# Two attentions of a two-model forward pass: output-weight halves subtracted one step after they are cast, and one chunk's queries turned ahead of the scores

## The reference

```python
def odd_mixer(h_lat, h_ctx, w_in, w_out, sink, cos, sin, ctx_out):
    q, k, v = odd_project(h_lat, w_in)
    qc, kc, vc = odd_project(h_ctx, w_in)
    q = apply_rope(q, cos, sin)
    k = apply_rope(k, cos, sin)
    y, yc = window_gqa_sink(q, k, v, qc, kc, vc, sink, ctx_out)
    return y @ w_out, ((yc @ w_out) if ctx_out else None)
```

## Time and profile before

| | |
|---|---|
| median of 3 runs | 1707.29 us (1706.27 to 1708.68) |
| the profiled execution, its own time | 1701.35 us |
| its span, first to last instruction | 1699.9 us |
| mean granted clock of TensorE | 0.977 |
| TensorE matmuls, busy | 1593.0 us, 94% |
| VectorE, busy | 1049.2 us, 62% |
| ScalarE, busy | 805.3 us, 47% |
| GpSimd, busy | 238.5 us, 14% |
| loads and stores | 257.27 MB, mean 151 GB/s |

### The profile page before, as it was taken

How to read it: one execution, slowest core, us unless ns; L and a number is a source line. 1 busy time by engine, 2 the same in 40 slices (tenths; PEclk the granted TensorE clock), 3 DMA queues, 4 the chain that set the end, 5 groups by cost and what they waited for, 6 DMA issues and landing times.

```text
span 1699.9 us, 26871 instructions
## 1 busy us (share of the span) xinstructions
PE 1593.0 (94%) x10834; PEld 1382.0 (81%) x10834; DVE 1049.2 (62%) x1939; ACT 805.3 (47%) x1514; POOL 238.5 (14%) x284
## 2 busy tenths in 40 slices
PE   5899979999999999979899997888999998899998
PEld 3788758877777888867799986777999887689996
DVE  3633755565354435778787767666677656667765
ACT  1322872433233323558455544555555555556553
POOL 1200430010010100002011101132111012321110
PEclk8999999999999999999999998899999998999999
DMA  9467022262564224020356453324455533245452
GB/s 383 151 255 276 11 71 114 77 254 117 217 253 173 99 99 149 11 91 25 149 178 218 175 189 103 130 95 141 158 190 181 189 133 119 75 155 193 174 209 76
DMA packets 39418, 257.27 MB, mean 151 GB/s; under 512 B 5504, under 2 KB 6784, under 8 KB 10496
## 3 DMA queue, kind: packets, MB, share of 16 engines
q1 hardware_dynamic: 36416, 249.61, 40.4%
q0 software_dynamic: 1296, 4.72, 0.8%
q10 hardware_dynamic: 1584, 1.23, 0.3%
HBM read 254.49 MB, written 1.05 MB: 150 GB/s over the span
## 4 chain that ended last, share of the span: by engine, by line
PE 81%; DVE 9%; ACT 6%; issue 2%; DMA 1%; POOL 1%; SPq 0%; DVEq 0%; ACTq 0%
PE ps L473 24%; PE ps L474 23%; PE ps L475 23%; PE ps L489 2%; PE ps L640 2%; PE ps L627 2%; DVE wl L1709 2%; PE ps L618 2%; ACT wh L1277 1%; ACT arena L1621 1%; PE ps L1043 1%; ACT arena L1348 1%; PE ps L515 1%; DMA raw<-in_ev_w_in 1%; PE ps L599 1%
## 5 line engine op out<-in xcount | busy, mean ns | idle before, releaser
L1709 DVE TENSOR_TENSOR wl<-raw,wh 128x1024 fp32r<-128x1024 f32 (+2 forms) x328 | 383.0, 1209 | 379.5 <-ACT wh L1277 378.9
L1277 ACT CAST wh<-raw 128x1024 fp32r<-128x1024 f32 (+1 forms) x338 | 332.6, 1033 | 517.1 <-PE ps L475 398.5
L473 PE MATMUL ps<-xh,wh 128*128 128x256 f32 (+1 forms) x1582 | 495.4, 313 | 8.3 <-ACT arena L1578 8.0
L474 PE MATMUL ps<-xl,wh 128*128 128x256 f32 (+1 forms) x1582 | 490.0, 310 | 0.0
L475 PE MATMUL ps<-xh,wl 128*128 128x256 f32 (+1 forms) x1582 | 489.9, 310 | 0.0
L473 PEld LDWEIGHTS ps<-xh,wh 128*128 128x128 f32 x1582 | 303.4, 192 | 33.2 <-issue 9.2
L473 PE MATMUL ps<-wh,xh 128*128 128x512 f32 (+2 forms) x844 | 306.6, 363 | 21.6 <-DVE xl L2275 6.8
L475 PEld LDWEIGHTS ps<-xh,wl 128*128 128x128 f32 x1582 | 303.4, 192 | 15.3
L474 PEld LDWEIGHTS ps<-xl,wh 128*128 128x128 f32 x1582 | 303.5, 192 | 15.0 <-issue 0.7
L474 PE MATMUL ps<-wl,xh 128*128 128x512 f32 (+2 forms) x844 | 301.9, 358 | 0.0
L475 PE MATMUL ps<-wh,xl 128*128 128x512 f32 (+2 forms) x844 | 301.7, 357 | 0.0
(11 more groups left out here) (210 smaller groups left out, 1805.0 us busy)
## 6 DMA issues: line engine op xcount, KB each, us to landing
raw<-in_ada SPq DMA_DIRECT2D x48, 1024.0 KB, 6.8
raw<-in_up SPq DMA_DIRECT2D x44, 1024.0 KB, 6.0
raw<-in_fin SPq DMA_DIRECT2D x44, 1024.0 KB, 4.8
raw<-in_down SPq DMA_DIRECT2D x22, 1024.0 KB, 4.9
raw<-in_fout SPq DMA_DIRECT2D x22, 1024.0 KB, 4.9
raw<-in_win SPq DMA_DIRECT2D x12, 1024.0 KB, 4.9
raw<-in_ev_w_in SPq DMA_DIRECT2D x9, 1024.0 KB, 6.7
raw<-in_wout SPq DMA_DIRECT2D x8, 1024.0 KB, 4.8
```

The costliest lines, as they stand in the source:

```text
L473: e.matmul(out, A[0], B[0], start=first, stop=False)
L474: e.matmul(out, A[0], B[1], start=False, stop=False)
L1277: e.copy(hi_of(j)[:, a:b], raw_of(j)[:, a:b]).then_inc(*S.hi.up((j, half)))
L1709: e.tensor_tensor(lo_of(j)[:, a:b], raw_of(j)[:, a:b], hi_of(j)[:, a:b].bitcast(F), ALU.subtract).then_inc(*S.lo.up((j, half)))
```

## The change

In both attentions, ScalarE casts a half of an early output-weight chunk in a step, and VectorE subtracts it in the step after. In the even attention only VectorE's place moves (steps 16, 18, 20, 22). In the odd attention chunks 0 and 1 of `od_w_out` are both split so, cast in steps 4, 6, 8 and 10 and subtracted in 5, 7, 9 and 11. So chunk 0 is no longer split ahead of the loop and chunk 1 no longer whole in step 4. VectorE's diagonals for the gates move to steps 12 and 14.

TensorE turns query chunk 1 before the scores of step 0, and only the product of chunk 3 stays in step 1. The copies of turned chunks 1, 2 and 3 are all made by ScalarE; those of chunk 1 stand before the loop, behind the fifth group of query tiles.

```diff
--- before.py
+++ after.py
@@ -445,7 +445,8 @@
     ATT2 = [Att2(l) for l in range(2)]
 
 
-    EARLY = {15 + 2 * i: (J["ev_w_out", i // 2], i % 2) for i in range(4)}
+    EARLY = {("ev", 15 + 2 * i): (J["ev_w_out", i // 2], i % 2) for i in range(4)}
+    EARLY |= {("od", 4 + 2 * i): (J["od_w_out", i // 2], i % 2) for i in range(4)}
 
 
 
@@ -572,7 +573,7 @@
                 take_turn((key, f))
                 wait_copied(b, (key, f))
 
-        def head_features(key, js, src, toks, wait):
+        def head_features(key, js, src, toks, wait, side=None):
 
             for j in js:
                 b = bank()
@@ -584,6 +585,8 @@
                 m.then_inc(*S.tr.up((key, j)))
                 BANK[key, j] = b
                 take_turn((key, j))
+                if side:
+                    SIDE[key, j] = side
                 wait_copied(b, (key, j))
 
         def gates(key, groups, at):
@@ -871,7 +874,7 @@
         def od_turned(i):
 
             head_features("oqt", [2 * i, 2 * i + 1], lambda t, j: QS1[:, t, 128 * j:128 * j + 128], t2,
-                          [(S.vec, ("oqk", (2 if i == 0 else 4 + 2 * i) + 1))])
+                          [(S.vec, ("oqk", (2 if i == 0 else 4 + 2 * i) + 1))], "act" if i else None)
 
         od_queries(1)
         head_features("okt", range(2), lambda t, j: KS[:, t, j, :, :].rearrange("p two d -> p (two d)"), t4, [(S.vec, ("oqk", 5))])
@@ -884,14 +887,14 @@
         def last_queries(i):
 
             nb[0] = 1
-            if i in (1, 2, 3):
+            if i == 1:
+                od_queries(3)
+            elif i in (2, 3):
                 od_turned(i)
-            if i == 1:
-                nb[0] = 1
-                od_queries(3)
 
         keys = [(S.ea if SIDE.get(("okt", j)) == "act" else S.ev, ("okt", j)) for j in range(2)]
-        span[:] = [6, 2]
+        span[:], nb[0] = [6, 2], 1
+        od_turned(1)
         attention1(ATT["od"], {0: [(S.ea, ("ova", 3)), *keys, *both_copied(0)]} | {4 * i: both_copied(2 * i) for i in (1, 2, 3)},
                    last_queries)
         span[:] = [0, 6]
@@ -1510,8 +1513,8 @@
 
         def first_weights(i):
             copies_vb(copy, 1, {1: (0, 1), 2: (2, 3)}.get(i, ()))
-            if i in EARLY:
-                weights_half(*EARLY[i])
+            if ("ev", i) in EARLY:
+                weights_half(*EARLY["ev", i])
 
         attention1(ATT["ev"], J["ev_w_in", 8], first_weights)
 
@@ -1537,22 +1540,24 @@
         for n, tiles in enumerate(QK1[0:5]):
             for tile in tiles:
                 qk(tile)
-            i = n - 2 if n > 2 else {0: 4, 1: 0}.get(n)
+            i = {0: 4, 1: 0, 3: 1}.get(n)
             if i is not None:
                 weights(after(J["od_w_in", i]))
             if n == 3:
                 copies_heads(copy, "okt", range(2), KT, 512)
                 copies_heads(copy, "oqt", [0, 1], QT1, 256, -0.125, free)
+            if n == 4:
+                copies_heads(copy, "oqt", [2, 3], QT1, 256, -0.125)
 
         def last_queries(i):
             if i == 1:
                 for tile in QK1[5]:
                     qk(tile)
-            elif i == 4:
-                weights(after(J["od_w_in", 3]))
+            elif ("od", i) in EARLY:
+                weights_half(*EARLY["od", i])
 
         def queries_turned(i):
-            if i in (1, 2, 3):
+            if i in (2, 3):
                 copies_heads(copy, "oqt", [2 * i, 2 * i + 1], QT1, 256, -0.125)
 
         attention1(ATT["od"], J["od_w_in", 3], last_queries, queries_turned)
@@ -2169,8 +2174,8 @@
             copies_vb(copy, 1, {1: (0, 1), 2: (2, 3)}.get(i, ()))
             if i in (5, 7, 9, 11):
                 next(diagonals)
-            if i in EARLY:
-                weights_half(*EARLY[i])
+            if ("ev", i - 1) in EARLY:
+                weights_half(*EARLY["ev", i - 1])
 
         attention1(ATT["ev"], beside)
 
@@ -2205,13 +2212,13 @@
                 for tile in QK1[5]:
                     qk(tile)
                     qk_rest()
-            elif i == 4:
-                weights(after(J["od_w_in", 3]))
-            elif i in (6, 8):
+            elif ("od", i - 1) in EARLY:
+                weights_half(*EARLY["od", i - 1])
+            elif i in (12, 14):
                 next(diagonals)
 
         def queries_turned(i):
-            if i in (1, 2, 3):
+            if i in (2, 3):
                 copies_heads(copy, "oqt", [2 * i, 2 * i + 1], QT1, 256, -0.125)
 
         attention1(ATT["od"], beside_od, queries_turned)
```

## The result

| | before | after |
|---|---|---|
| median (runs) | 1707.99 us (4) | 1684.84 us (4) |
| lowest to highest | 1706.27 to 1709.97 | 1683.21 to 1686.60 |
| the profiled execution | 1701.35 us | 1684.03 us |
| its span | 1699.9 us | 1682.7 us |
| mean granted clock | 0.977 | 0.977 |

The ratio is 0.9861, 95% interval 0.9847 to 0.9876: 23.7 us of 1707.99, between 21.2 and 26.1. The medians are 23.2 us apart, the two profiled executions 17.3. The forecast was 1689.6 us with a range from 1685.0; the median fell 0.16 us under its low end. Timed once more, the changed kernel had 1685.44 us, and over all eight executions 1685.38, which lies just inside: on which side of the end the median fell is chance, that it lies over 4 us under the forecast is not. The profiled execution of 1684.03 us is 0.3 us from the 1683.7 that the prediction's sum gave for it.

A forecast was written before the change was run, and what follows sets the result against it. The prediction took TensorE, busy 94% of the span, as the bound. Its terms 7.9 + 7.6 + 0.3 + 1.9 = 17.7 us, subtracted from the median 1707.29, gave 1689.6 us, own range 1686 to 1694, with rivals 1685 to 1700.

The forecast's parts named there:

- First attention, 7.9 us: Step 16 to the gates: 8.9 us of TensorE idle goes, less 1.0 us for ScalarE's longer steps.
- Turn ahead of the scores and VectorE's subtraction moved, 7.6 + 0.3 = 7.9 us: Second attention before step 4: 0.55 and 4.54 us idles and 2.5 us of halved clock go; VectorE's copy saves 0.3.
- Odd halves, 1.9 us: Second attention, step 4 to the gates: 2.6 us of TensorE idle goes, less 0.7 us for longer steps.
- the bound's 0.7 us: Second attention: cost taken for eight longer steps with halves, between bounds of nothing and 1.9 us.
- Diagonals and DMA queue at nothing: Second attention: VectorE's slack covers the moved diagonals, 1.7 us without cover; later raw buffers have over 20 us of cover.
- Some 1.5 us for the scatter of runs: Whole kernel: allowance added to terms at their bounds (gain 15.4 to 19.4) to give the forecast's own range, 1686 to 1694.
- time lost after 802.35 that was not lost before: Behind the second attention's gates: a sign that would show the forecast wrong; no loss was expected there.
- The rule on the clock: Skill text held against the change: brief idles between matmul groups, as banks are cycled, can make TensorE's clock swing.
- a clock that falls in both attentions: Rival, steps 16 to 23 and 4 to 11: clock falls at idles between 1.98 and 4.54 us; 1730.6 us, chance 0.03.
- Casts on the path: Rival, both attentions: ScalarE's pace rules eight cast steps, costing 8.3 us in place of 1.7; 1696.2 us, chance 0.17.
- the turn bringing nothing: Rival, second attention: TensorE still idles before the last product, a copy being behind something on ScalarE; 1697.2 us, chance 0.06.
- both halves on the path: Rival, both attentions: eight halves cost 2.26 us each, together 18.1, cancelling the gain; 1706.0 us, chance 0.04.

The follow-up runs named there:

- 8.79 alone: Kernel before with only the even attention's edit, VectorE's halves moved to steps 16, 18, 20, 22: median 1693.64 us, ratio 0.9932.
- the halves alone: Kernel before with only the odd attention's output-weight halves split over steps 4 to 11 and diagonals in 12 and 14: median 1698.84 us, ratio 0.9970.

## Why the prediction was right, and where it failed

**First attention, 7.9 us: 8.66 measured** (8.79 alone). The 10.7 us of waits went, as the earlier trace rows had it. The 1.0 us set aside for ScalarE's longer steps was 1.06 us of idle in one place, so 7.84 us of idle went; the other 0.82 us is busy time, 32.84 to 32.02.

**Turn ahead of the scores and VectorE's subtraction moved, 7.6 + 0.3 = 7.9 us: 7.84** (13.65 us from the first scores to those of step 4, in place of 21.49). The table at 724.68 shows each piece: no idle, the product at 1.00. That the 1.56 us idle before step 4 would stay was right: 1.54. One reading was off without effect: the 26 matmuls in 3.00 us of the earlier trace rows are more than the product's remaining 24, which start 0.12 us apart in the timeline; the sum used 0.12. The split between the terms was not clean, as the halves alone already bring back the clock and half of the idle.

**Odd halves, 1.9 us: 1.93.** The idle of 0.89 us at 778.69 is the bound's 0.7 us.

**Diagonals and DMA queue at nothing:** both so. Without its cover the diagonals' move was priced at 1.7 us; undone, it cost 0.06 us.

**The step that failed** is the one behind the sum. "The median of the three runs is 1707.29, 5.9 above it; I subtract from the median" took the 5.9 us between the profiled execution and the median as a constant of the measurement, equal on both sides. It is not: 126 executions of the kernel before lie between 1701.35 and 1711.79 us, median 1707.04, and the profiled one is the shortest of them all. The changed kernel's profiled execution lies 0.8 us under its median. The sum gave 1683.7 for it, and 1683.7 + 0.8 = 1684.5 is within 1 us of the measured 1684.84; with 5.9 in place of 0.8 it became 1689.6. What the distance of before was made of is shown in part: between its two profiled executions, 7.0 us apart, 5.9 us lie behind the odd gates, in stretches with the same idle and a lower clock. Filling the idles there takes 5.2 us of its median and some 3 of the other. What decides in which execution the clock stays down stays open. "Some 1.5 us for the scatter of runs" was the same mistake in the range: three runs 2.4 us apart, with a profiled one 4.9 us under the lowest of them, were already evidence of a spread of over 7 us, of which a change in either direction may keep or lose a part.

**A term put at nothing.** Behind 802.35 the prediction expected no change, and named "time lost after 802.35 that was not lost before" as a sign of being wrong. That sign came: 1.6 us more of TensorE's idle at 1486.08, with the copies fixed on ScalarE. The 0.8 us by which the first attention's term was too small and 0.4 us gained ahead of its step 16 made up for most of it, so it is in part luck that the sum met the profiled execution within 0.3 us.

**The rule on the clock.** The prediction held the rows against it ("Against: 8.9 us of idles in 41.74 at 1.00"), with a chance of 0.03 for a clock that falls in both attentions. In the stretches of the changed kernel shown above it stayed at 1.00, so the rival did not come. But its point of decision, between 1.98 and 4.54 us, was wrong: the clock fell behind 1.66 us in one kernel and behind 1.98 us in another, and stayed at 1.00 behind 2.25 us in a third and, in the second stack of the changed kernel, behind 3.40 us at 1122.06. The length of the idle alone does not decide.

**The rivals.** Casts on the path (1696.2), the turn bringing nothing (1697.2) and both halves on the path (1706.0) are each refuted by a row: 1.06 us of idle behind the first attention's four casts and 0.89 behind the second's, no idle before the product, 0.2 us of waits ahead of line 1720.

## What to carry to other kernels

Before a difference of profiled executions is subtracted from a median, ask where the profiled execution stands among the runs: when it lies outside them, the gap is scatter, and its cause may change with the edit. A wait between two engines that share a step's work goes away by giving the second engine the work one step later, as long as there is slack for the longer steps; here 8.9 us of idle became 1.1. When a kernel keeps a few idles of some us on TensorE, add to the range what a halved clock behind them costs, since the same idle may have that or not. And compare the stretches behind the edit too: a few instructions less on one engine brought it beside another one 750 us later.

## What the runs showed of the hardware that was not expected

- The same program, with the same 50 us of TensorE idles behind the odd gates, took 897.55 us there in one execution and 903.41 in another; the difference was in stretches at a granted clock of 0.80 to 0.89 in one and 0.90 to 1.00 in the other.
- 4.3 us of useless work at about 565 us made the changed kernel 8.2 us longer, and 17.4 us of it made it 18.5 us longer.
- Filling idles until the mean granted clock of the changed kernel rose from 0.977 to 0.989 brought 3.3 us behind the odd gates (899.02 to 895.71). The clock withheld behind the odd gates fell by 13.8 us (26.9 to 13.1, over pieces of 5 us), so three quarters of what the filling gave back there saved nothing that the time shows. Where the rest is covered was not looked into.
- VectorE's two subtractions of 128x1024 took 4.56 us where GpSimd's began beside the first of them, and 2.36 us where GpSimd's began 1.76 us into VectorE's; GpSimd's two took 6.33 in place of 5.24. TensorE's idle behind them was 4.71 us in place of 3.12.
